# A two-block transformer kernel on one core: the expert gates' table is put together in DRAM instead of on TensorE

## What is computed

```python
def peer_ffn(x, w_query, keys_1, keys_2, expert_down, expert_up):   # 8 heads, 128 x 128 experts, top 16
    q = (x @ w_query).reshape(b, s, 8, 2, 128)
    s1 = einsum("bshc,hkc->bshk", q[..., 0, :], keys_1)
    s2 = einsum("bshc,hkc->bshk", q[..., 1, :], keys_2)
    v1, i1 = top_k(s1, 16); v2, i2 = top_k(s2, 16)
    cand_score = v1[..., :, None] + v2[..., None, :]               # 256 candidates
    cand_idx = i1[..., :, None] * 128 + i2[..., None, :]
    top_score, pos = top_k(cand_score, 16)
    experts = take_along_axis(cand_idx, pos)
    gates = softmax(top_score)
    # per token: sum over heads and picks of gate * gelu(expert_down[e] . x) * expert_up[e]
```

## Time and profile before

| | us |
|---|---|
| median of 3 runs | 1586.87 (1586.11 to 1588.28) |
| the profiled execution, its own time | 1586.05 |
| its span, first to last instruction | 1584.2 |
| PE busy | 1531.3 |
| DVE busy | 1028.0 |
| ACT busy | 836.2 |
| POOL busy | 351.3 |

### The profile page before, as it was taken

The page is one execution under the profiler, slowest core; times in us unless marked ns, Lnnn a source line. Parts: engine busy times, 40 slices in busy tenths (PEclk is TensorE's granted clock), DMA queues, the critical chain, the costliest instruction groups (busy, mean ns, idle before and its releaser), DMA issues.

```text
span 1584.2 us, 28579 instructions
## 1 busy us (share of the span) xinstructions
PE 1531.3 (97%) x11138; PEld 1437.0 (91%) x11138; DVE 1028.0 (65%) x1792; ACT 836.2 (53%) x1638; POOL 351.3 (22%) x403
## 2 busy tenths in 40 slices
PE   7799999999988989999999999999999999999998
PEld 6389999999988989999999999999999888888886
DVE  4255567555576875476999976777775555555554
ACT  4166455444456543445444457777775554545454
POOL 1133431000155463321465540001112000000000
PEclk9899999999998999999999999999999999999999
DMA  9732455555433442356445554444444656666664
GB/s 216 224 107 81 133 184 169 178 183 186 160 108 113 146 139 77 106 168 195 147 159 174 174 184 151 146 136 145 137 144 162 196 191 196 189 197 194 192 196 137
DMA packets 76771, 254.20 MB, mean 160 GB/s; under 512 B 11375, under 2 KB 15293, under 8 KB 76509
## 3 DMA queue, kind: packets, MB, share of 16 engines
q1 hardware_dynamic: 76397, 251.71, 49.9%
q0 software_dynamic: 240, 0.66, 0.2%
HBM read 250.23 MB, written 1.84 MB: 159 GB/s over the span
## 4 chain that ended last, share of the span: by engine, by line
PE 80%; DVE 12%; DMA 2%; ACT 2%; POOL 2%; issue 1%; SPq 1%; POOLq 0%; DVEq 0%; ACTq 0%
PE bank L675 78%; DVE wl L1661 4%; DVE big L1661 2%; POOL big L2341 2%; DMA big<-in_w1k 1%; ACT big L1236 1%; DVE big L1664 1%; ACT wh L1236 1%; DVE big L2187 1%; DVE big L2198 1%; DVE big L2194 1%; DVE big L2183 1%; DVE big L2204 1%; DVE big L2191 1%; PE bank L984 1%
## 5 line engine op out<-in xcount | busy, mean ns | idle before, releaser
L1661 DVE TENSOR_TENSOR wl<-raw,wh 128x1024 fp32r<-128x1024 f32 (+4 forms) x459 | 531.5, 1159 | 399.5 <-ACT wh L1236 398.9
L1236 ACT ACTIVATE wh<-raw 128x1024 fp32r<-128x1024 f32 (+1 forms) x459 | 482.2, 1053 | 351.3 <-PE bank L675 333.1
L675 PE MATMUL bank<-gw,wh 128*128 128x256 f32 x3504 | 651.3, 287 | 2.4 <-DVE big L1664 2.4
L675 PEld LDWEIGHTS bank<-gw,wh 128*128 128x128 f32 x3504 | 547.4, 193 | 3.0 <-DVE big L1664 2.8
L675 PE MATMUL bank<-gw,wl 128*128 128x256 f32 x1752 | 497.7, 284 | 6.4 <-POOL wl L2341 5.0
L675 PEld LDWEIGHTS bank<-gw,wl 128*128 128x128 f32 x1752 | 336.8, 192 | 8.0 <-issue 6.3
L675 PE MATMUL bank<-xw,wh 128*128 128x256 f32 x1696 | 321.9, 290 | 9.9 <-ACT wh L1236 7.5
L675 PE MATMUL bank<-wh,xw 128*128 128x512 f32 x1056 | 326.9, 391 | 0.0
L675 PEld LDWEIGHTS bank<-xw,wh 128*128 128x128 f32 x1696 | 267.9, 194 | 16.8 <-ACT wh L1236 7.8
L1236 ACT ACTIVATE big<-bank 128x256 f32<-128x256 f32 (+23 forms) x326 | 118.5, 373 | 260.6 <-PE bank L675 222.7
L2341 POOL TENSOR_TENSOR wl<-raw,wh 128x384 fp32r<-128x384 f32 (+3 forms) x131 | 175.6, 1346 | 336.9 <-ACT wh L1236 336.9
(11 more groups left out here) (136 smaller groups left out, 1107.7 us busy)
## 6 DMA issues: line engine op xcount, KB each, us to landing
raw<-in_wst SPq DMA_DIRECT2D x455, 512.0 KB, 3.6
big<-toeplitz SPq DMA_DIRECT2D x8, 256.0 KB, 14.2
big<-in_w1k SPq DMA_DIRECT2D x4, 512.0 KB, 18.1
big<-in_w1v SPq DMA_DIRECT2D x4, 512.0 KB, 19.4
big<-in_xT SPq DMA_DIRECT2D x4, 256.0 KB, 5.0
raw<-in_wst SPq DMA_DIRECT2D x4, 256.0 KB, 4.7
big<-in_keys SPq DMA_DIRECT2D x1, 1024.0 KB, 5.5
out<-big SPq DMA_DIRECT2D x4, 256.0 KB, 2.4
```

The lines of the kernel that those rows point to most:

```text
L675: return e.matmul(o, a, b, start=first, stop=last, skip_group_check=True)
L1236: return e.activation(o, x, f, **kw)
L1661: return e.tensor_tensor(o, a, b, f)
```

## The change

The table of gates (16384 experts x 256 tokens, 16.8 MB) now lies in DRAM. SP clears it with 64 DMAs of 256 KB, behind the loads of units 16 to 31 and 122 to 169. The softmax is taken for two heads at a time inside the top-16 stage (ACT's Exp with the negated maximum as bias, DVE's reciprocal, POOL's multiplication), and POOL computes each pick's address (`places`). POOL then adds the gates into the table with 256 indirect accumulating DMAs ("puts"), one for each head, half of the tokens and rank: 128 single floats to 128 computed addresses. Head 0's 32 puts stand one a slot in slots 212 to 243, the other 224 one a tick from slot 247 on. SP loads the table back, 128 KB ahead of each up unit's weights, into five buffers (`GTILE`), and DVE multiplies it into `ACTS` three slots before the unit is used. The build on PE, ACT, DVE and POOL is gone, and the down units use three banks in turn to their end instead of two.

```diff
@@ -72,9 +72,7 @@
         return u - QU
     if u < DN + 4:
         return (u + 1) % 2 if u > QU + 4 else 0
-    if u < DN + 48:
-        return (u - DN - 4) % 3
-    return (u - DN) % 2
+    return (u - DN - 4) % 3
...
@@ -157,13 +156,15 @@
...
-        ET = misc[:, 0:512].rearrange("p (n t) -> p n t", n=2)
-        GATE = misc[:, 512:768]
-        IOTA = misc[:, 768:896]
+        IDX = misc[:, 0:256].bitcast(I32)
+        GV = misc[:, 256:512]
+        ZERO = misc[:, 512:768]
+        TOK = misc[:, 768:800].rearrange("p (t k) -> p t k", t=2)
+        TOKI = misc[:, 800:832].bitcast(I32).rearrange("p (t k) -> p t k", t=2)
         RS2 = misc[:, 896:900]
         RS4 = misc[:, 900:902]
-        VG = [misc[:, 900:1028], misc[:, 1028:1156], ones[:, :], ident[:, :]]
-        TG = misc[:, 1156:1412]
+        NGT = 5
+        GTILE = [misc[:, 256 * i:256 * i + 256] for i in range(NGT)]
...
+        table = nc.dram_tensor("gates", [128 * 128 * T, 1], F32).ap()
...
@@ -530,6 +534,10 @@
         TURNS = [(s, s + 1) for s in range(0, 24, 2)]
         FEATURES_AT = {22: 1, 26: 3, 28: 4, 30: 5}
         WINDOW_AT = (0, 11, 23, 36)
+        CLEAR_AT = [*range(16, 32), *range(CK, CK + 48)]
+        PUT_AT = [4 * (22 + j) + 2 if j < 32 else 4 * 57 + j - 32 for j in range(256)]
...
+                        if u in CLEAR_AT:
+                            clear(CLEAR_AT.index(u))
+                def clear(i):
+                    if i == 0:
+                        e.wait_ge(*zeG.at(0))
+                    e.dma_start(table[65536 * i:65536 * i + 65536, :].rearrange("(p a b) c -> p a (b c)", a=2, b=256),
+                                ZERO[:, None, :].broadcast_to([128, 2, 256])).then_inc(*s_zero.sent(i))
+                def gates(n):
+                    if n == 0:
+                        for tile in range(2):
+                            e.wait_ge(*s_put[tile].at((7, 15)))
+                    if n >= NGT:
+                        e.wait_ge(*gmD.at(n - NGT))
+                    e.dma_start(GTILE[n % NGT], table[32768 * n:32768 * n + 32768, :].rearrange("(p t) c -> p (t c)", t=T)).then_inc(
+                        *s_gt[n % NGT].sent(n))
...
@@ -652,9 +677,11 @@
...
-                weights(191, UNITS)
+                weights(191, UP)
+                for n in range(128):
+                    gates(n)
+                    weights(UP + n, UP + n + 1)
...
@@ -1182,37 +1209,8 @@
...
-                def topk_side():
-                    b = banks[7]
-                    yield from clock.until(190 + 56, 0)
-                    e.wait_ge(*tkD.at((7, "red", 1)))
-                    e.wait_ge(*scA.at(7))
...
-                            z = e.transpose(b[:, 256 * n + 128 * tile:256 * n + 128 * tile + 128],
-                                            src[:, tile, :, :].rearrange("p h k -> p (h k)"), ident[:, :])
-                    z.then_inc(*tkP.sent("ids"))
...
-                def build_side():
-                    for g in range(NB):
-                        yield from clock.until(BUILD + g, 0)
-                        b = banks[(2, 7)[g % 2]]
-                        if g == 0:
-                            e.wait_ge(*evA.at(DN + 45))
-                        if g > 1:
-                            e.wait_ge(*fiA.at(g - 2))
-                        for j in range(4):
-                            e.wait_ge(*vgA.at((g, j)))
-                            mm(b[:, half(j)], HOT[g % 4][:, j, 0, :].bitcast(F32), VG[j]).then_inc(*buP.sent((g, j)))
...
@@ -1318,19 +1316,12 @@
                         act(GB2[:, u - PGB, :], ps, AF.Tanh, scale=0.5).then_inc(*evA.sent(u))
...
-                        m = min(max(4 * (u + 1 - BUILD), 0), T)
                         e.wait_ge(*unit.at(u))
...
-                        if m < T:
-                            z = act(ACTS[:, n, m:T], ps[:, m:T], AF.Gelu)
-                        if m > 0:
-                            if n > BUILD - DN:
-                                e.wait_ge(*dnG.at(n - 1))
-                            z = act(TG[:, 0:m], ps[:, 0:m], AF.Gelu)
-                        z.then_inc(*evA.sent(u))
+                        act(ACTS[:, n, :], ps, AF.Gelu).then_inc(*evA.sent(u))
...
@@ -1555,43 +1546,19 @@
...
                 def topk_side():
-                    yield from clock.until(190 + 53, 0)
-                    e.wait_ge(*tkD.at("sub"))
-                    act(TS, TS, AF.Exp).then_inc(*tkA.sent("exp"))
...
-                def build_scale_side():
-                    for g in range(NB):
-                        yield from clock.until(BUILD - 1 + g, 1)
-                        e.wait_ge(*hotD.at(g))
...
-                                e.wait_ge(*buP.at((g - 1, j)))
-                            act(VG[j], HOT[g % 4][:, j, 1, :].bitcast(F32), AF.Copy,
-                                scale=GATE[:, 4 * g + j:4 * g + j + 1]).then_inc(*vgA.sent((g, j)))
-
-                def build_fill_side():
-                    for g in range(NB):
-                        yield from clock.until(BUILD + g, 2)
-                        n = BUILD + g - DN
-                        g4 = banks[(2, 7)[g % 2]][:, :].rearrange("p (t e) -> p e t", e=128)
-                        e.wait_ge(*foD.at(g))
-                        act(ACTS[:, n:128, 4 * g:4 * g + 4], g4[:, n:128, :], AF.Copy).then_inc(*fiA.sent(g))
+                    for p in range(4):
+                        t = 26 * (2 * p + 1) + 25
+                        yield from clock.until(QU + 5 + t // 4, t % 4)
+                        e.wait_ge(*tkG.at((2 * p + 1, "neg")))
+                        for tile in range(2):
+                            for h in (2 * p, 2 * p + 1):
+                                x = TS[:, tile, h, :]
+                                act(x, x, AF.Exp, bias=M8[:, tile, h:h + 1],
+                                    accum_out=S8[:, tile, h:h + 1]).then_inc(*tkA.sent((p, tile, h)))
...
                 def up_high(n):
                     s = (n + 4) % 8
-                    if n == 0:
-                        e.wait_ge(*foD.at(NB - 1))
-                        e.wait_ge(*fiA.at(NB - 1))
-                    if n >= BUILD - DN:
-                        e.wait_ge(*dnG.at(n))
+                    e.wait_ge(*gmD.at(n))
...
@@ -2204,6 +2170,11 @@
...
+                def gate_scale(p):
+                    hs = slice(2 * p, 2 * p + 2)
+                    e.wait_ge(*tkA.at((p, 1, 2 * p + 1)))
+                    e.reciprocal(R8[:, :, hs], S8[:, :, hs]).then_inc(*tkD.sent((p, "recip")))
...
@@ -2239,45 +2212,17 @@
...
-                def build_fold_side():
-                    for g in range(NB):
-                        yield from clock.until(BUILD + g, 1)
-                        n = BUILD + g - DN
-                        t = slice(4 * g, 4 * g + 4)
-                        x = ACTS[:, 0:n, t]
...
-                        tt(x, x, banks[(2, 7)[g % 2]][:, :].rearrange("p (t e) -> p e t", e=128)[:, 0:n, :],
-                           ALU.mult).then_inc(*foD.sent(g))
...
-                def build_hot_side():
-                    for g in range(NB):
-                        yield from clock.until(BUILD - 2 + g, 1)
...
-                        tt(HOT[g % 4], IOTA[:, None, None, :].broadcast_to([128, 4, 2, 128]),
-                           ET[:, :, 4 * g:4 * g + 4].rearrange("p n t -> p t n")[:, :, :, None].broadcast_to([128, 4, 2, 128]),
-                           ALU.is_equal).then_inc(*hotD.sent(g))
...
                 def up_side():
                     for n in range(128):
+                        yield from clock.until(DN + 125 + n, 1)
+                        x = ACTS[:, n, :]
+                        e.wait_ge(*evA.at(DN + n))
+                        e.wait_ge(*s_gt[n % NGT].at(n))
+                        tt(x, x, GTILE[n % NGT], ALU.mult).then_inc(*gmD.sent(n))
...
@@ -2376,15 +2320,6 @@
...
-                    elif DN <= u < UP:
-                        n = u - DN
-                        m = min(max(4 * (u + 1 - BUILD), 0), T)
-                        if m > 0:
...
-                            tt(x, x, TG[:, 0:m], ALU.mult).then_inc(*dnG.sent(n))
...
@@ -2521,15 +2456,32 @@
...
+                def places(h):
+                    x = FP[:, :, h, :]
+                    e.wait_ge(*tkD.at((h, "red", 1)))
+                    tt(x, x, FJ[:, :, h, :], ALU.add).then_inc(*tkG.sent((h, "sum")))
+                    e.wait_ge(*tkG.at((h, "sum")))
+                    tt(x, x, TOK, ALU.add).then_inc(*tkG.sent((h, "tok")))
+                    e.wait_ge(*tkG.at((h, "tok")))
+                    e.tensor_copy(IDX.rearrange("p (t h k) -> p t h k", t=2, k=16)[:, :, h, :], x).then_inc(*tkG.sent((h, "idx")))
+                def gates(p):
+                    hs = slice(2 * p, 2 * p + 2)
+                    e.wait_ge(*tkD.at((p, "recip")))
+                    tt(GV.rearrange("p (t h k) -> p t h k", t=2, k=16)[:, :, hs, :], TS[:, :, hs, :],
```

(71 more changed lines are left out.)

54 lines of the change are left out of this document (11 added, 43 removed).

## The result

The changed kernel takes 1874.99 us (median of 4, 1873.87 to 1876.98) against 1586.49 (1586.01 to 1588.28): ratio 1.182, 95% interval 1.180 to 1.184. The forecast was 1566, with a range up to 1640.

What follows compares the result with a forecast made beforehand. PE was taken as the bound, with DVE setting the pace in the top-16 stage. 1586.05 - 56.8 - 1.3 (transposes) + 5 + 8 + 22.4 + 2 = 1565.4, plus 0.8 to the median: 1566 us; range 1535 to 1640.

Steps and rivals of the forecast that it cites:

- What bounds the kernel: Whole kernel: PE is full and sets the pace, except in the top-16 stage, where DVE does.
- its matmuls gone: Down units with the build: 64 slots each lose 0.89 us of PE's time for the build's products, -56.8 us.
- The 224 puts: Ahead of up unit 0: at 1.10 us each on POOL the puts end 22.4 us late; they fit at 1.00.
- A rule weighed: Puts beside DVE's split: if held like POOL's split, 0.26 us each on average, 58 us, time 1624; by the skill, nothing.
- Rival 2: Ahead of the up stage: puts become the bound, slower from 1.19 us a put, up to 1709 us; chance 0.30.
- rival 3: Puts are held by something besides their own length: the read port (1624 us) or the DMA engines; chance 0.11.
- What POOL's new work costs in the stage: Top-16 stage: small instructions and early puts on POOL delay PE, +8 us, between 3 and 20.
- Exp +5: Top-16 stage: four ACT excursions for the softmax, with two table loads each, instead of one: +5 us, between 0 and 11.
- Clears: 64 clears of 256 KB fall where weights have slack: 0 us, with 5 for the range.
- ACT waited for weights only 5 times: Whole kernel: ACT's 5 waits for weights, 18.2 us in all, taken as sign of slack for the clears.
- DVE's product is 0.50 us ... 76%, no bound: Up stage: the gate product on top of DVE's 1.55 of 2.71 us a slot costs 0.
- A PE that stood still comes back slowly: Behind PE's wait ahead of the up stage: a lower granted clock, +2 us.

Runs made afterwards that it cites:

- experiment 2: Changed kernel without the 256 puts, and DVE's product of up unit n+1 issued ahead of the low part of unit n: 1545.97 us, ratio to before 0.974.
- experiment 6: Changed kernel with each put a direct accumulating DMA of the same 128 floats to fixed places, without a list of addresses: 1588.4 us.
- experiment 9: Changed kernel with only the first 112 of 256 puts, and DVE's product one up unit ahead: 1577.67 us, ratio to before 0.995.
- experiment 5: Changed kernel with the 256 puts overwriting instead of adding: 1872.9 us.
- experiment 3: Changed kernel with DVE's split subtracting a PSUM bank, so one SBUF input, from unit DN+50 to the last down unit: 1802.6 us.
- experiment 4: Changed kernel with all 256 puts from slot 247 on, none in the top-16 stage: 1912.3 us.
- experiment 8: Kernel of experiment 2 with ACT's 16 exponentials replaced by Gelu, so its table never changes: 1545.4 us.
- experiment 7: Kernel of experiment 2 with 48 of the 64 clears moved from slots 122 to 169 to slots 261 to 308: 1543.9 us.
- experiment 10: Whole changed kernel, all 256 puts, with DVE's product one up unit ahead: 1838.71 us, ratio to before 1.159.

## Why the prediction was wrong, step by step

- **What bounds the kernel, and "its matmuls gone", -56.8: right.** From copy 250 to 335 the kernel before takes 302.3 us, that of experiment 2 244.5: 57.8 less.
- **"The 224 puts", +22.4: the step that failed.** The mechanism was right (POOL's time before up unit 0, the chain tile, product, ACT, PE), and its threshold of 1.00 us agrees with the runs: at one put every 0.91 us they fit (experiment 6), and the 80 late ones that were said to fit at 2.88 did (experiment 9). The size was not: 1.10 us a put was taken, up to 1.74, from direct DMAs of other shape. A put takes 1.54 and leaves 0.30 behind it, 1.85 in all, by 0.11 above the upper bound; the bound counted pieces and an irregular side, and had no row for the addition (0.58 us, experiment 5) and none for the pause of POOL between two. And 74 of them met a split and ran at 2.88. By the prediction's own sum: 224 x (1.85 - 1.00) = 190, and 74 x 1.03 = 76, 266 us instead of 22; PE's wait was 260.5.
- **"A rule weighed": the wrong side of it was believed.** The trace before showed POOL's split of 384 held by DVE's, 1.66 for 1.02 us. A put was to be held for 0.26 us on average if it was held at all; it is held for 1.03, in 74 of 224 puts, one for each slot (experiment 3). The Trainium skill (SBUF — State Buffer, Who interferes with whom) says that a VectorE instruction with two SBUF inputs blocks GpSimd's reads. The put reads its addresses from SBUF, and experiment 3 agrees with that sentence. What the page infers of descriptor generation, that it needs only the write side, does not carry over to an indirect DMA. That the read of the addresses is the part that stands still is likely but not shown: what is held lies in the first 0.1 us of a put, and the direct puts of experiment 6, which have no addresses to read, keep their pace beside the same split; but they differ in more than that.
- **Rival 2, "the puts become the bound", 0.30: what happened**, beyond its upper end of 1709. With rival 3's read port on top and the two terms below, it gives the measured time.
- **"What POOL's new work costs in the stage", +8, and Exp +5, between 3 and 31 together: +38.9.** Early puts 23.5 (experiment 4), tables 0.7 (experiment 8), which leaves 14.7 for the small instructions of POOL, without a kernel of their own. The sum had POOL as full as DVE with puts of 1.1 us; they were 1.55 to 2.2 there, and POOL's splits behind them 1.57 for 1.02.
- **Clears, kept at 0 "with 5 for the range": +4.7** (experiment 7), inside the range. "ACT waited for weights only 5 times" was true and beside the point: the trace shows a round trip through DRAM of the delta stage that came late. In the window 552 to 562 us the DMA share is 0.52 before and with the clears moved, 0.71 in after and 0.95 without puts. Behind it DVE waits for the tile that comes back from `diag_out` for 4.8 us in after, and for 0.6 with the clears moved (0.7 before; waits of 562 to 600 us):

```profile
DVE big L1627 <- DMA big<-diag_out: 4.8, 1, 4.8
```
```profile
DVE big L1627 <- DMA big<-diag_out: 0.6, 1, 0.6
```

- **"DVE's product is 0.50 us ... 76%, no bound", at 0: +34.7.** The product takes 0.42 and DVE is at 66%: the busy time was even lower than forecast. It is the order that costs. The step asked whether DVE has room and not what the product waits for and who waits for it: (2.995 - 2.72) x 126 slots is 34.7 us, and experiment 10 gives 36.3 back.
- **"A PE that stood still comes back slowly", +2: right in kind.** The granted clock was 0.50 in the wait, 0.83 in the 10 us behind it, then 1.00.

The terms as measured: 1586.5 - 57.8 + 4.7 + 38.9 + 260.5 + 34.7 = 1867.5 us, against 1875.0. Of the 7.5 that are missing, 4.2 belong to the one split that stands behind four puts, for which PE waited 2.7 us: copies 250 to 320 take 205.8 us in after and 201.6 in experiment 2 (206.4 in experiment 9, which has these puts too).

## What to carry to other kernels

A price for 256 instructions in a row is to be measured before anything is built on it: here 0.1 us a put was 22 us of the result, and no row of the trace was of its kind (direct DMAs of 0.54 to 0.60 us stood for one of 1.54). An instruction that is added to an engine with room can still cost a tenth of each slot, if it closes a loop between two engines: write the loop down, start to start, and put the new instruction one unit ahead of it. And instructions in a row beside a periodic one of another engine that holds them can fall into step with it, as here, where the hold ends late enough for the next to begin inside the next split; the cost is then the whole hold, each time, not the mean.

## What the runs showed of the hardware, unexpected

- An indirect accumulating DMA of 128 single floats holds GpSimd for 1.54 us with a pause of 0.30, and for 2.57 where it begins just inside a VectorE subtraction of 1024 columns with two SBUF inputs (1.23 us); with one of them in PSUM it is 1.54 again.
- Such a subtraction holds an indirect DMA only if it is already running when the DMA begins: one that began 0.01 us ahead of it kept its 1.54, the 76 that began in one ended 1.41 to 1.44 us behind its end.
- Without the addition it is 0.96 us (1.31 where it meets that subtraction); direct, with the addition and 128 places, one by itself is 0.85 to 0.91, and a row of them goes at one every 0.89, at a DMA share of 0.99.
- Plain indirect DMAs sent back to back every 1.26 us slowed TensorE to one product in 2.8 us, with no wait shown, while the DMA engines were busy for 1.9% of their time; two in 2.88 us did not. What lies behind it is open.
